# Input normed by token tile before it is turned, low-rank and attention gates with high and low columns side by side, compression inputs stored in order

## The chip, the cores and the metric

The program runs on one core of a Trainium2 chip. The metric is the device time of one execution in microseconds (us), the median of three executions; less is better. The core's engines are named as in the profile: PE (TensorE) multiplies, its weight loads are PEld; DVE (VectorE), ACT (ScalarE) and POOL (GpSimd) compute on tiles; SP (SyncE) issues most of the DMAs.

## What is computed

Two transformer-like blocks over 512 tokens of 1024 channels, in fp32. The first block has a gated linear attention layer (GLA) and a sparse attention layer (NSA), the second a stick-breaking attention with a pooling branch. Cut to what the change touches:

```python
def rms_norm(x, g):
    y = xf * lax.rsqrt(jnp.mean(xf * xf, axis=-1, keepdims=True) + NORM_EPS)
    return (y * g.astype(jnp.float32)).astype(x.dtype)

# layer 0, GLA: w_in is 1024 x 3088, 16 of its columns are the low-rank gate
h = rms_norm(x, pre_norm[0])
q, k, v, glr, z = split(h @ w_in)
gk = log_sigmoid(glr @ w_gk_up + b_gk) / 16
...
# layer 1, NSA: 48 gate columns; k and v compressed over blocks of 32 tokens
gates = sigmoid(gl + b_gate)                  # 512 x 48
kcmp = compress(kc, pe_k, ck_w1, ck_w2)       # 31 blocks, 4 groups
vcmp = compress(vc, pe_v, cv_w1, cv_w2)
s = einsum('bghtd,bgcd->bghtc', qb, kcmp)     # then softmax over blocks
...
```

## The kernel before

**How a product is made.** Each fp32 operand is kept as a high part (rounded to the type fp32r, in `w_hi`, `act_hi`) and a low part (the rest, in `w_lo`, `act_lo`). A product of fp32 accuracy takes three matmuls: high by high, low by high, high by low. Activations stand channels first: `act_hi` and `act_lo` are [128, 8, 512], eight slices k of 128 channels by 512 tokens. Weights are streamed in chunks of 256 columns (1 MB), numbered through the whole program: chunk 0 is `C_GLR`, 1 and 2 are `C_Q`, 3 and 4 `C_K`, 27 is `C_GL`, 28 to 31 `C_NQ`. Chunk c goes through buffer c % 2 of `raw`, `w_hi` and `w_lo`: SP loads it, once the low part of the chunk two back is done (`lo_done`), ACT makes the high part in two halves (`split_high`, L654), POOL the low part (`split_low`, L581), PE waits for each half (`weights_ready`) and writes PSUM banks 2u and 2u+1 (u = c % 2), ACT or DVE takes the banks and frees them (`bank_free`). The first chunks are handled apart.

**Order.** Every engine runs its own list in the order of the code and waits on semaphores. Nothing is scheduled by a planner; the order is written out by hand.

**The start.** SP loads x in two halves by channels (L400), then eleven small vectors (L404), `w_up`, and three chunks (L418). PE turns the raw x, eight slices of four 128x128 transposes (L1279), DVE copies them to `xT` (L1805). ACT squares x by token (L782); the sums are spread over all partitions by small matmuls on PE (L1287), and ACT makes `rstd` from them (L681, L682). Then, slice by slice, DVE makes `tmp` = xT * gain * rstd (L1822), ACT rounds it to `act_hi` (L691), DVE subtracts to `act_lo` (L1787). PE follows the slices (loop at L1292 on): for each k three matmuls of the low-rank chunk, which is loaded and multiplied 128 columns wide though 16 are used (L1296), and four of the first query chunk (L1305); the 16 matmuls with that chunk's low part come at the end (L1310). DVE makes both low parts of chunks 0 and 1 (`first_low`, L1813). The next product, chunk 2, has the gate's second factor in its middle: four matmuls with a contraction of 16 rows (`low_rank_up`, L1321).

**NSA.** `kv_high` (L862, ACT) and `kv_low` (L2031, DVE) split the gathered keys or values `kv_tok2` into `kv_hi` and `kv_lo`, which the compression's matmuls read (L1443). In both, elements are walked in the order group, block, position: `kv_tok2` is read in memory order, `kv_hi` and `kv_lo` are written with a step of 512 bytes between neighbours. Between `kv_low` and the values' arrival ACT copies the value banks to `kv_tok2` (L897). The gates' chunk C_GL is loaded whole, its 48 columns take three matmuls for each k (L1480), ACT applies bias and sigmoid (L921), PE turns the result (L1496), DVE copies it (L2072). The compressed scores (`c_score`, L1508) are 16 matmuls with a contraction of 64 rows and 32 result columns for each of four j, into banks 4 and 5; the two groups of a pair use the upper and lower half of the partitions.

## Time and profile before

| what | us |
|---|---|
| median of three executions | 1302.6 (1301.8 to 1305.51) |
| the profiled execution, whole | 1305.59 |
| its span in the trace | 1303.8 |
| PE busy within the span | 1258.7 (97%) |
| ACT, DVE, POOL busy | 576.2, 652.9, 400.4 |
| mean granted PE clock | 0.985 of full speed |

The trace shows the instructions of the profiled execution, from the start of its span. A group of matmuls is given its busy time with overlaps, so the spacing of starts, not the duration, says what one costs. "PEclk" is the clock that PE was granted, 1.00 for 2.4 GHz and 0.50 for 1.2 GHz. The idle time in brackets stands before the instruction on its own engine, with what ended it.

### The profile page before, as it was taken

The page shows a single profiled execution, that of the slowest core. Times are in us where ns is not written, and L with a number is a line of the kernel's source. Part 1 is how long each engine was busy: PE and PEld are TensorE (multiplying, and loading weights), DVE is VectorE, ACT ScalarE, POOL GpSimd, SP SyncE. Part 2 cuts the span into 40 slices and gives each one's busy share as a digit, 9 for nine tenths or more (in the row PEclk, how much of TensorE's full clock was granted, in tenths as well). Part 3 has the DMA queues.
Part 4 walks back from the last instruction along what each step waited for, and adds up shares of the span by engine and source line. Part 5 has one row for each costly group of instructions (what it writes and reads, how often), then busy time and mean ns, then how long its engine had stood idle before and what let it go on. Part 6 is the DMA issues. An engine that isn't in the chain of part 4 may idle for free.

```text
span 1303.8 us, 19513 instructions
## 1 busy us (share of the span) xinstructions
PE 1258.7 (97%) x7802; PEld 1040.4 (80%) x7802; DVE 652.9 (50%) x1212; ACT 576.2 (44%) x1086; POOL 400.4 (31%) x194
## 2 busy tenths in 40 slices
PE   6999998999989999999999999999999999999998
PEld 5799875998877765656699988888887788888898
DVE  6297534577815547698747033333333391102534
ACT  4435312353532137788846344445354411434333
POOL 1453411305652212010020422222222354444441
PEclk8999998999999999999999999999999999999999
DMA  5524500715465311110013232222111223333221
GB/s 172 181 77 144 179 1 33 241 55 162 130 133 94 77 38 42 24 34 2 1 33 98 69 94 65 65 65 65 61 60 60 80 97 97 97 98 109 80 86 65
DMA packets 130209, 109.68 MB, mean 84 GB/s; under 512 B 36162, under 2 KB 127424, under 8 KB 130128
## 3 DMA queue, kind: packets, MB, share of 16 engines
q1 hardware_dynamic: 130128, 108.54, 28.0%
q8 instruction: 58, 0.95, 0.3%
q14 instruction: 23, 0.19, 0.0%
HBM read 106.43 MB, written 2.10 MB: 83 GB/s over the span
## 4 chain that ended last, share of the span: by engine, by line
PE 69%; issue 17%; POOL 7%; DVE 4%; ACT 2%; DMA 0%; POOLq 0%; DVEq 0%; ACTq 0%
PE banks L1153 33%; POOL w_lo L581 6%; PE banks L1144 6%; PE banks L1176 5%; PE banks L1703 3%; PE banks L1555 3%; PE banks L1572 3%; PE banks L1587 3%; PE banks L1610 2%; PE banks L1241 2%; PE banks L1666 2%; PE banks L1717 1%; PE banks L1747 1%; PE banks L1120 1%; DVE w_lo L1813 1%
## 5 line engine op out<-in xcount | busy, mean ns | idle before, releaser
L581 POOL TENSOR_TENSOR w_lo<-raw,w_hi 128x1024 fp32r<-128x1024 f32 x158 | 389.8, 2488 | 811.8 <-ACT w_hi L654 811.7
L1153 PE MATMUL banks<-act_hi,w_hi 128*128 128x512 f32 x704 | 280.9, 399 | 2.1 <-POOL w_lo L581 2.1
L1153 PE MATMUL banks<-act_lo,w_hi 128*128 128x512 f32 x704 | 276.5, 393 | 0.0
L1153 PE MATMUL banks<-act_hi,w_lo 128*128 128x512 f32 x704 | 276.5, 393 | 0.0
L654 ACT ACTIVATE w_hi<-raw 128x1024 fp32r<-128x1024 f32 x168 | 168.0, 1050 | 123.4 <-PE banks L1153 91.6
L1153 PEld LDWEIGHTS banks<-act_hi,w_hi 128*128 128x128 f32 x704 | 133.6, 190 | 32.3 <-issue 5.0
L1153 PEld LDWEIGHTS banks<-act_lo,w_hi 128*128 128x128 f32 x704 | 133.3, 189 | 28.4
L1153 PEld LDWEIGHTS banks<-act_hi,w_lo 128*128 128x128 f32 x704 | 133.3, 189 | 28.2 <-issue 1.4
L1144 PE MATMUL banks<-w_hi,act_hi 128*128 128x256 f32 x384 | 109.4, 285 | 1.6 <-POOL w_lo L581 1.6
L1144 PE MATMUL banks<-w_hi,act_lo 128*128 128x256 f32 x384 | 108.8, 283 | 0.0
L1144 PE MATMUL banks<-w_lo,act_hi 128*128 128x256 f32 x384 | 108.8, 283 | 0.0
L968 ACT ACTIVATE prob<-prob,wstat 128x128 f32<-128x128 f32 (+3 forms) x128 | 70.8, 554 | 34.4 <-DVE wstat L2120 34.2
L2229 DVE TENSOR_TENSOR tmp<-banks,zh 128x512 f32<-128x512 f32 x8 | 5.5, 692 | 141.4 <-PE banks L1717 141.4
L1144 PEld LDWEIGHTS banks<-w_hi,act_hi 128*128 128x128 f32 x384 | 73.7, 192 | 2.1 <-issue 1.1
L1144 PEld LDWEIGHTS banks<-w_lo,act_hi 128*128 128x128 f32 x384 | 73.7, 192 | 0.0
L1144 PEld LDWEIGHTS banks<-w_hi,act_lo 128*128 128x128 f32 x384 | 73.7, 192 | 0.0
L1572 PEld LDWEIGHTS banks<-ident,prob 128*128 128x128 f32 x320 | 35.9, 141 | 33.3 <-issue 25.4
L1176 PE MATMUL banks<-w_hi,act_hi 128*128 128x256 f32 x192 | 56.4, 294 | 3.9 <-DVE act_lo L1787 2.3
L2120 DVE CUSTOM_DVE_ANT_0 prob<-banks,key_mask 128x128 f32<-128x128 f32 (+3 forms) x128 | 57.1, 484 | 3.7 <-PE banks L1555 3.5
L1176 PE MATMUL banks<-w_lo,act_hi 128*128 128x256 f32 x192 | 55.6, 289 | 0.0
L1176 PE MATMUL banks<-w_hi,act_lo 128*128 128x256 f32 x192 | 55.5, 289 | 0.0
L1572 PE MATMUL banks<-ident,prob 128*128 128x128 f32 x320 | 48.5, 282 | 5.7 <-ACT probT L981 3.8
(378 smaller groups left out, 2431.8 us busy)
## 6 DMA issues: line engine op xcount, KB each, us to landing
raw<-w_in SPq DMA_DIRECT2D x32, 1024.0 KB, 5.7
raw<-gla_w_in SPq DMA_DIRECT2D x13, 1024.0 KB, 5.4
raw<-nsa_w_in SPq DMA_DIRECT2D x32, 256.0 KB, 4.5
raw<-nsa_w_in SPq DMA_DIRECT2D x7, 1024.0 KB, 5.2
...
```

What stands on the lines that cost most here:

```text
L581: pool.tensor_tensor(w_lo[:, u, k], raw[:, u, k], w_hi[:, u, k].bitcast(F32), ALU.subtract).then_inc(lo_done, 1)
L654: act.activation(w_hi[:, u, k], raw[:, u, k], ACT.Copy).then_inc(hi_done, 1)
L968: act.activation(p, p, ACT.Exp, scale=-1.0, bias=wstat[:, u % 4, 0, half:half + 1], accum_out=wstat[:, u % 4, 1, half:half + 1]).then_inc( ...
L1144: mm = pe.matmul(b[:, t * CW:(t + 1) * CW], x[:, k, tok], w[:, u, k, :], start=(k == 0 and n == 0), stop=(k == KT - 1 and n == 2))
L1153: mm = pe.matmul(b[:], w[:, u, k, m * P:(m + 1) * P], x[:, k, :], start=(k == 0 and n == 0), stop=(k == KT - 1 and n == 2))
L1176: mm = pe.matmul(zone, x[:, k, tok], w[:, u, k, :], start=(start and n == 0), stop=(stop and n == 2), skip_group_check=True)
L1241: mm = pe.matmul(bank[2 * u + m][:, tok], w[:, u, k, m * P:(m + 1) * P], x[:, k, tok], start=(half == 0 and k == 0 and n == 0), stop=(k == ...
L1555: mm = pe.matmul(bank[2 * (u % 2) + half][:, 0:keys], qT[rows, i, t * P:(t + 1) * P], kT[rows, i // 4, 0:keys], start=True, stop=True)
L1572: mm = pe.transpose(bank[4 + half][:, k * P:(k + 1) * P], prob[:, u % 3, half, k * P:(k + 1) * P], ident[:])
L1587: mm = pe.matmul(bank[6][half * NDH:(half + 1) * NDH, 0:P], v_tok2[:, k, w, g * NDH:(g + 1) * NDH], probT[:, u % 2, half, k * P:(k + 1) * ...
L1703: mm = pe.matmul(blocks(z_banks, a, st, skip=jt - st), (tri_r if jt == st else minus_r)[:], blocks(part, a, jt), start=False, stop=(jt == ...
L2120: last = dve.tensor_tensor_reduce(prob[:, u % 3, half, 0:keys], bank[2 * (u % 2) + half][:, 0:keys], key_mask[:, S - keys:S], -1.0, -NEG, ...
```

## The change

It has four parts, and all the rest of the program stays as it was.

1. **The start.** x is loaded by token tile (four DMAs), the small vectors are issued from ACT's queue. ACT squares a token tile as it comes and makes one factor for each token (`x_root`); DVE scales the tile in place of tokens (`xn_tok`); PE turns the normed tiles, one pass of 32 transposes, into all eight banks, which are then read where they stand: ACT writes `act_hi` from the bank times the gain, DVE `act_lo` from the bank times the gain less `act_hi`. Ahead of that PE does 28 transposes of a constant tile whose result nobody reads. POOL, not DVE, makes the low part of chunk 1.
2. **The low-rank gate.** Its 16 columns (32 are loaded, 128 KB) stand as 32 high and 32 low columns in `glr_w`; one matmul with `act_hi` makes both partial results on 64 rows, one with `act_lo` adds to the first 32. `w_up` holds its 16 rows twice, with zeros between, so that the second factor's contraction of 64 rows also adds the two.
3. **The attention gates** in the same way: 64 columns are loaded, high and low side by side in `w_hi`; the two halves are added by a matmul with `pair_ident` that also turns them; bias by DVE, then the sigmoid by ACT.
4. **Compression.** `kv_hi` and `kv_lo` are walked in their own memory order and `kv_tok2` is read with a step of 8 elements (32 bytes). `kcmp2` holds the compressed keys of a pair of groups as two diagonal blocks, so that `c_score` is eight matmuls of 128 rows and 64 columns.

```diff
@@ sync @@
-            for half in range(2):
-                sp.dma_start(x_tok[:, :, half * S:(half + 1) * S],
...
+            for t in range(TT):
+                sp.dma_start(x_tok[:, t], A["x"][t * P:(t + 1) * P, :]).then_inc(x_landed[t], 16)
+            sp.dma_start(glr_raw[:], cols(w1, G_R, 32)).then_inc(glr_landed, 16)
...
+                        for half, landed in enumerate((first_landed, raw_landed[1])):
+                            k = slice(KT // 2 * half, KT // 2 * (half + 1))
+                            sp.dma_start(raw[:, 1, k], cols(m, at)[:, k]).then_inc(landed, 16)
...
+                elif c0 == C_GL:
+                    sp.wait_ge(lo_done, 2 * C_GL - 2)
+                    sp.dma_start(raw[:, C_GL % 2, :, 0:NDH], cols(m, at, NDH)).then_inc(raw_landed[C_GL % 2], 16)
@@ gpsimd @@
+            pool.memset(w_up[0:64, :], 0.0)
...
-            pool.wait_ge(lo_done, 2 * C_Q + 2)
-            split_range(C_Q + 1, C_KC)
+            split_low(C_Q, 1)
+            pool.wait_ge(lo_done, 2 * C_K)
+            split_range(C_K, C_KC)
...
+                    pool.tensor_tensor(w_hi[:, u, k, NDH:2 * NDH], raw[:, u, k, 0:NDH], w_hi[:, u, k, 0:NDH].bitcast(F32),
+                                       ALU.subtract).then_inc(lo_done, 1)
@@ scalar @@
+            for tiles in (range(3), range(3, 4)):
+                for t in tiles:
+                    act.wait_ge(x_landed[t], 16)
+                    ins = act.activation(sq_junk[:, t], x_tok[:, t], ACT.Square, accum_out=x_sum[:, t:t + 1])
...
+                link(act.activation(x_root[:, t], x_sum[:, t], ACT.Ln, scale=1.0 / D, bias=eps_col[:]))
+                act.activation(x_root[:, t], x_root[:, t], ACT.Exp, scale=-0.5).then_inc(start_rooted, 1)
+            act.wait_ge(glr_landed, 16)
+            act.activation(glr_w[:, :, 0, :], glr_raw[:], ACT.Copy).then_inc(hi_done, 2)
...
+            act.wait_ge(first_landed, 16)
+            first_high(1, 0)
+            act.wait_ge(vec_ready, 1)
+            for k in range(KT):
+                act.wait_ge(start_turned, k + 1)
+                act.activation(act_hi[:, k], start_bank(k), ACT.Copy, scale=vcol("pre0", k)).then_inc(act_hi_done, 1)
+                if k == 2:
+                    act.wait_ge(raw_landed[1], 16)
+                    first_high(1, 1)
+            act.wait_ge(raw_landed[0], 32)
+            first_high(0, 0)
+            first_high(0, 1)
...
-            act.activation(glr_t[:], bank[1][0:16, :], ACT.Copy).then_inc(bank_free[1], 1)
+            act.activation(glr_t[0:64, :], bank[1][0:64, :], ACT.Copy).then_inc(bank_free[1], 1)
             act.sem_inc(bank_free[0], 1)
...
-                    last = act.activation(by_block(kv_hi, part), kv_even(part), ACT.Copy)
+                    last = act.activation(kv_hi[:, part], kv_even(part), ACT.Copy)
...
-            act.activation(gates_t[:], bank[2 * u + 1][0:48, :], ACT.Sigmoid, bias=gate_bias[:]).then_inc(bank_free[2 * u + 1], 1)
+            act.activation(gate_parts[:], bank[2 * u + 1][:], ACT.Copy).then_inc(bank_free[2 * u + 1], 1)
...
-            untaken(C_NQ, 2)
+            untaken(C_NQ)
+            act.wait_ge(gate_summed, 1)
+            act.activation(gates[:].rearrange("p t n -> p (t n)"), gates[:].rearrange("p t n -> p (t n)"), ACT.Sigmoid)\
+                .then_inc(gate_ready, 1)
+            untaken(C_NQ + 1)
@@ tensor @@
+            for n in range(N_WARM):
+                pe.transpose(bank[7][:, n % 4 * P:(n % 4 + 1) * P], ones[:], ident[:])
...
+            for t in range(TT):
+                pe.wait_ge(start_scaled, t + 1)
+                for k in range(KT):
+                    mm = pe.transpose(start_bank(k)[:, t * P:(t + 1) * P], xn_tok[:, t, k * P:(k + 1) * P], ident[:])
...
+                mm = pe.matmul(bank[1][0:64, :], glr_w[:, k].rearrange("p a n -> p (a n)"), act_hi[:, k, :], start=(k == 0),
+                               stop=(k == KT - 1))
...
+                if k == KT - 1:
+                    mm.then_inc(bank_full[1], 1)
...
+                    pe.matmul(bank[4 + h][:], w_up[0:64, h * P:(h + 1) * P], glr_t[0:64, :], start=True, stop=True)\
...
-                mm = pe.transpose(bank[7][:, t * 48:(t + 1) * 48], gates_t[:, t * P:(t + 1) * P], ident[0:48, 0:48])
+                mm = pe.matmul(bank[7][:, t * 48:(t + 1) * 48], gate_parts[:, t * P:(t + 1) * P], pair_ident[:], start=True, stop=True)
...
+                        mm = pe.matmul(bank[4][:, at:at + 2 * NCP], qT[:, 2 * j + ii, t * P:(t + 1) * P], kcmp2[:, j // 2, :],
+                                       start=True, stop=True)
@@ vector @@
+            for t in range(TT):
+                dve.wait_ge(start_rooted, t // 3 + 1)
+                dve.tensor_scalar(xn_tok[:, t], x_tok[:, t], x_root[:, t:t + 1], None, ALU.mult).then_inc(start_scaled, 1)
...
+                dve.wait_ge(act_hi_done, k + 1)
+                dve.scalar_tensor_tensor(act_lo[:, k], start_bank(k), vcol("pre0", k), act_hi[:, k].bitcast(F32), ALU.mult,
+                                         ALU.subtract).then_inc(h_ready, 1)
...
+            dve.wait_ge(gate_ready, 1)
```

Where instructions now stand, at three places. On PE, the start of its list before, up to the first matmuls of the products (`tok_squares` are the sums of squares):

```order
L1279 MATMUL banks<-ident,x_tok 128x128 x32
L1282 MATMUL banks<-ident,vec_rows 128x94
L1287 MATMUL banks<-ident,tok_squares 128x128 x8
L1296 MATMUL banks<-act_hi,w_hi 128x512
L1296 MATMUL banks<-act_hi,w_lo 128x512
L1296 MATMUL banks<-act_lo,w_hi 128x512
```

and now:

```order
L1333 MATMUL banks<-ident,ones 128x128 x28
L1335 MATMUL banks<-ident,vec_rows 128x94
L1340 MATMUL banks<-ident,xn_tok 128x128 x32
L1362 MATMUL banks<-act_hi,w_hi 128x512
L1362 MATMUL banks<-act_hi,w_lo 128x512
L1362 MATMUL banks<-act_lo,w_hi 128x512
```

The turning moved behind the norm, the constant transposes stand where the turning stood, and the sums' matmuls are gone. On PE, the end of this first stage before, with the waits:

```order
L1310 MATMUL banks<-act_hi,w_lo 128x512 [waits lo_done]
L1310 MATMUL banks<-act_hi,w_lo 128x512 x7
L1310 MATMUL banks<-act_hi,w_lo 128x512 [waits lo_done]
L1310 MATMUL banks<-act_hi,w_lo 128x512 x7
L1153 MATMUL banks<-act_hi,w_hi 128x512 [waits lo_done,bank_free0]
```

and now (L1349 and L1350 are the low-rank gate's last two, L1211 the first of chunk 2):

```order
L1362 MATMUL banks<-act_lo,w_hi 128x512
L1349 MATMUL banks<-act_lo,glr_w 32x512
L1350 MATMUL banks<-act_hi,glr_w 64x512
L1211 MATMUL banks<-act_hi,w_hi 128x512 [waits lo_done,bank_free0]
L1211 MATMUL banks<-act_hi,w_lo 128x512
```

The 16 matmuls between the low-rank gate and chunk 2 are gone from there, so its last result stands directly ahead of the wait for `bank_free0`. On ACT, from the table load on, before:

```order
L676 ACT_TABLE_LOAD
L782 ACTIVATE sq_junk,tok_squares<-x_tok 128x512 x8
L681 ACTIVATE rstd<-banks,eps_col 128x512
L682 ACTIVATE rstd<-rstd 128x512
L654 ACTIVATE w_hi<-raw 128x1024 x2
L691 ACTIVATE act_hi<-tmp 128x512 x8
L791 ACTIVATE glr_t<-banks 16x512
```

and now, behind eleven DMA issues:

```order
L703 ACT_TABLE_LOAD
L806 ACTIVATE sq_junk,x_sum<-x_tok 128x1024 x3
L811 ACTIVATE x_root<-x_sum,eps_col 128x3
L812 ACTIVATE x_root<-x_root 128x3
L806 ACTIVATE sq_junk,x_sum<-x_tok 128x1024
L811 ACTIVATE x_root<-x_sum,eps_col 128x1
L812 ACTIVATE x_root<-x_root 128x1
L814 ACTIVATE glr_w<-glr_raw 128x8x32
L819 ACTIVATE w_hi<-raw 128x1024
L826 ACTIVATE act_hi<-banks,vec 128x512 x3
L819 ACTIVATE w_hi<-raw 128x1024
L826 ACTIVATE act_hi<-banks,vec 128x512 x5
```

The norm's factors come in two steps ahead of the first weights, and the second half of chunk 1's high part stands behind the third slice.

## Rows read from the trace of the kernel before

**Rows 1.** Waits of PE, 0 to 60 us: in total, times, longest.

```profile
PE banks L1279 <- DMA x_tok<-x: 6.3, 1, 6.3
```

**Rows 2.** Timeline of the start: begins, lasts (us), engine, line, operation [idle before].

```profile
0.81 1.28 ACT L676 ACT_TABLE_LOAD   x1 [0.81 <-PEq L2366]
...
1.86 0.81 SPq L404 DMA_DIRECT2D vec_rows<-pre_norm  x2
...
5.50 0.25 SPq L404 DMA_DIRECT2D vec_rows<-gla_head_norm  x1
...
4.95 0.10 POOL L574 MEMSET rstd<- 128x1 f32 x1
...
20.20 0.77 PE L1296 MATMUL banks<-act_hi,w_hi 128*128 128x512 f32 x1 [4.78 <-DVE act_lo L1787]
...
34.31 0.59 ACT L791 ACTIVATE glr_t<-banks 16x512 f32<-16x512 f32 x1 [5.86 <-PE banks L1296]
...
35.02 3.79 PE L1310 MATMUL banks<-act_hi,w_lo 128*128 128x512 f32 x16
38.64 0.39 PE L1153 MATMUL banks<-act_hi,w_hi 128*128 128x512 f32 x1
```

**Rows 3.** Groups by line, 0 to 38.7 us: busy us, mean ns, idle before.

```profile
L1822 DVE SCALAR_TENSOR_TENSOR tmp<-xT,vec,rstd 128x512 f32<-128x512 f32 x8 | 6.0, 752 | 0.7 <-ACT rstd L682 0.5
...
L581 POOL TENSOR_TENSOR w_lo<-raw,w_hi 128x1024 fp32r<-128x1024 f32 x2 | 4.8, 2400 | 30.9 <-ACT w_hi L654 30.9
```

**Rows 4.** Stretches: length, busy us of PE, PEld, DVE, ACT, POOL, PE clock, DMA.

```profile
7.00:8.00 1.00, 1.00 (x6) 1.00 (x5) 0.58 (x1) 1.00 (x4) 0.00 (x0) 1.00 1.06 383
11.00:12.00 1.00, 1.00 (x11) 1.00 (x10) 1.00 (x2) 0.47 (x2) 0.00 (x0) 1.00 1.09 372
23.00:24.00 1.00, 1.00 (x4) 0.81 (x3) 1.00 (x2) 0.35 (x1) 0.00 (x0) 0.50 1.05 359
```

**Rows 5.** Nearest prices: timeline of ACT, then a DVE group by shape.

```profile
265.99 1.05 ACT L741 ACTIVATE y_tok<-x_tok 128x1024 f32<-128x1024 f32 x1
...
267.48 0.20 ACT L707 ACTIVATE x_root<-x_root 128x1 f32<-128x1 f32 x1
...
L2135 DVE TENSOR_SCALAR prob<-prob,wstat 128x512 f32<-128x512 f32 x16 | 7.8, 486 | 2.4 <-DVE wstat L2132 1.1
```

**Rows 6.** Line L1321 (ns min/median/max, first and last start), a stretch behind it.

```profile
L1321 PE MATMUL banks<-glr_t,w_up x8: 587/588/692, 44.2 to 47.3; 16*128 16x512 f32 x8
...
48.30:51.70 3.40, 3.40 (x10) 2.67 (x9) 1.56 (x4) 0.00 (x0) 0.00 (x0) 0.51 1.09 386
```

**Rows 7.** Compression: timeline of ACT, DVE and PE.

```profile
314.69 3.90 ACT L862 ACTIVATE kv_hi<-kv_tok 128x1024 fp32r<-128x1024 f32 x2 [8.96 <-DVEq L2052]
...
330.86 2.01 ACT L654 ACTIVATE w_hi<-raw 128x1024 fp32r<-128x1024 f32 x2 [0.30 <-issue]
...
318.89 6.15 DVE L2031 TENSOR_TENSOR kv_lo<-kv_tok,kv_hi 128x1024 fp32r<-128x1024 f32 x2 [4.29 <-ACT kv_hi L864]
...
329.93 0.29 PE L1443 MATMUL banks<-w_hi,kv_hi 128*128 128x256 f32 x1
...
339.23 0.36 PE L1144 MATMUL banks<-w_hi,act_hi 128*128 128x256 f32 x1 [0.78 <-POOL w_lo L581]
```

**Rows 8.** Attention gates: line L1480, then timeline of ACT and PE.

```profile
L1480 PE MATMUL banks<-act_hi,w_hi x8: 397/397/401, 373.6 to 378.5; 128*48 128x512 f32 x8
...
378.31 2.00 ACT L654 ACTIVATE w_hi<-raw 128x1024 fp32r<-128x1024 f32 x2 [5.05 <-DMA raw<-nsa_w_in]
...
381.94 0.47 PE L1153 MATMUL banks<-act_hi,w_hi 128*128 128x512 f32 x1 [2.13 <-POOL w_lo L581]
```

**Rows 9.** Timeline of PE: values, gates turned, compressed scores.

```profile
394.54 1.89 PE L1490 MATMUL banks<-w2v,tmp 128*128 128x64 f32 x16
396.37 0.45 PE L1496 MATMUL banks<-ident,gates_t 48*128 48x48 f32 x4
...
409.63 1.97 PE L1508 MATMUL banks<-kcmpT,qT 64*128 64x32 f32 x32
```

232 lines of the change are left out of this document (117 added, 115 removed).

## The prediction

> **What bounds the kernel now.** I read the waits of PE first, then the timeline of the start, then the stretches with their clock, then the groups by line for prices. PE is the engine that ends the kernel: behind its first products it stands still only in short gaps, so what PE loses or saves there moves the end one for one. Its two long waits are at the start: 6.3 us for x [rows 1] and, after turning, 4.78 us for the first low slice of the activations; the first product begins at 20.20, chunk 2 at 38.64 [rows 2]. Full-speed matmuls of 512 columns start 0.226 us apart (16 from 35.02 to 38.64, 3.62 / 16 [rows 2]). The 72 of the first stage would need 16.3 us; they take 18.4, since PE begins them at half clock: four starts in a microsecond at 23 us, clock 0.50 [rows 4]. That is 2.1 us lost.
>
> **The change part by part: the start.** Three chains meet at the first product.
>
> ACT: eleven DMA issues come ahead of its table load. SP's eleven run from 1.86 to 5.75 [rows 2], some 0.35 each, so on ACT from 0.8 to 4.6; the table load of 1.28 [rows 2] ends at 5.9. Three squares of 1024 columns at 1.05 and the roots: one square with its root is 1.69 us from 265.99 to 267.68 [rows 5], so the roots alone are 0.64, and three tiles are ready at 6.0 + 3.15 + 0.64 = 9.8, the fourth at 11.5. The 256 columns of `glr_raw` cost some 0.4 (a quarter of 1024 and its start-up, my estimate), half a chunk's high part 1.05, as the square of the same size: 12.9. POOL's half of the low part is 2.40 [rows 3]: 15.4.
>
> PE and DVE: constants are ready at 5.05 [rows 2], now with one memset more, 5.6. The 28 constant transposes go at the pace of today's first ones, seven in a microsecond [rows 4]: 4.0, to 9.6; the vectors' transpose, its copy and DVE's bias step make 10.8. Now DVE scales four tiles. No row has this; 512 columns scaled in SBUF take 0.49 [rows 5], so 1024 at most 0.97 and less by one start-up: I take 0.8. With the price of the two-source form as upper bound (0.75 for 512 [rows 3], 1.5) it is 6.0 for four, not 3.2. So the last tile is scaled at 14.0 and its first slice turned at 14.2; `act_hi` (0.63, near 0.6 of a bank copy [rows 2]) makes 14.8, `act_lo` at 0.75 [rows 3] 15.6. The first product starts at **15.7**, where the two chains meet almost; from 15.0 (scaling at half my price) to 18.4 (at its bound, + 2.8). The later slices come 0.75 apart and PE needs 1.36 for each slice's six matmuls alone, so they stay ahead. The second half of the low part (behind the third slice, about 19.6) is needed after 32 matmuls, at 22.9.
>
> Then 64 matmuls, 8 less than now (8 x 0.226 = 1.8), at full clock: 14.5, to 30.2. That the clock is full is a choice. The clock row says 1.00 for all of the start, but the transposes of 7 to 8 us start at seven in a microsecond and those of 11 to 12 at eleven [rows 4]; PE went faster after 5 us that held transposes only. So transposes raise its pace here, and the new start has 60 of them, with idle stretches of a microsecond at most ahead of the product. The Trainium skill says the opposite: "TensorE: Matmul & The Clock Gate", Part 4, holds that transposes do not count as activity for the clock. By it the 28 constant ones would do nothing and the 2.1 us would stay lost; the pace in the two rows above speaks against it, and I give the rule a chance of its own below.
>
> A new wait: chunk 2 needs bank 0 free, which ACT signals after its copy of the low-rank result, 0.59 [rows 2]. Today 16 matmuls (L1310) cover it: the copy starts at 34.31 and chunk 2 at 38.64. Now the low-rank matmul is the last one, and PE waits for the copy and the hand-overs on both sides of it, which I put at 0.2 together: **0.8**. ACT is free by then. Chunk 2 thus starts at 31.0, not 38.64: **-7.6** (4.5 for the earlier start, 1.8, 2.1, less 0.8). What was queued behind chunk 2 is covered: its high part follows the slices on ACT (about 23), its low part on DVE is done at 25.4. The ACT copy of the first queries now stands behind chunk 3's high part, needed only when chunk 3 ends its wait 15 us later: nothing.
>
> **The second factor.** The eight instructions of L1321 keep their columns, so their time. Behind them the clock is 0.51 over the 3.4 us from 48.3 to 51.7 [rows 6], after 3 us of matmuls that use 16 rows: half of it, 1.6 us or so, is lost. With 64 rows the array is used four times as much. No row shows 64-row matmuls of this length; gain between 0 and 1.6. I take **-1.6**, since nothing else but these rows of 16 stands ahead of the fall.
>
> **Compression.** ACT's two `kv_hi` take 3.90, DVE's two `kv_lo` 6.15; behind them come the value copies, and the next chunk's high part starts at 330.86 [rows 7]. POOL's four halves follow that, and PE waits for them: 0.78 at 339.23 is one of three such waits [rows 7]. 128x1024 in plain order is 1.05 on ACT [rows 5] against 1.95. The high part cannot start before the product ahead of it ends, at 329.93 [rows 7]: at most 0.9 is to be had, and it is had if the chain shortens by a microsecond. Bounds 0 and -0.9; I take **-0.9**, since only one of three streams keeps a step. The Trainium skill speaks against this part: "SBUF — State Buffer", under "Door 1: The DMA port swizzle", says that consecutive accesses in one 16-byte line run at full rate and each new line costs; the new order reads at 32-byte steps, so by the page reading would cost what writing costs now. The trace has no such read. By it this term is 0 and the sum 0.9 smaller.
>
> **Gates.** Three matmuls for each of eight k, whose first ones start at 373.6 to 378.5 [rows 8] (0.70 for three, 0.233 each), become two: 1.9 less on PE. But behind them PE waits 2.13 us, to 381.94, for a chain that starts with chunk 28's DMA, for which ACT waited 5.05 us [rows 8]. The load is released by chunk 26's low part, which no edit touches. So the 1.9 turns into a longer wait: **0**, from -0.3 to +1.7 (if the wait of four us costs one more stretch at half clock). The turning was 4 instructions in 0.37; now 4 fp32 products, each two instructions as L1490, whose 16 take 1.83 [rows 9]: 8 x 0.114 = 0.9, **+0.5**. The new waits: ACT holds for DVE's sum before the sigmoid, with chunk 30's high part queued behind it; that comes some 5 us later (about 400 to 402, low part to 406) and PE needs it at the end of chunk 29, near 409. DVE waits for the sigmoid, to about 400, and its next input from PE comes at 403. Both are covered.
>
> **Compressed scores.** 32 instructions in 1.90 become 16 of L1490's shape, 16 in 1.83 [rows 9]: four times -0.07, **-0.3**. If they kept the pace of today's small ones it would be four times -0.95, so the bounds are -0.3 and -3.8. DVE's mask becomes one instruction, off the path.
>
> **Sum.** -7.6 - 1.6 - 0.9 + 0.5 - 0.3 = -9.9. Against the profiled execution: 1305.6 - 9.9 = 1295.7. That execution is 3.0 above the median of the three; the same shift on the median gives 1302.6 - 9.9 = **1292.7**.
>
> **The rivals.** (1) *Cold products*: the clock at the first product is half, as the skill's rule has it, and the sum is 2.1 smaller: 1294.8. For it: today's products did start cold. Against: the pace of the transposes. (2) *Late start*: scaling at its bound puts the product at 18.4, or the 1024 short pieces of `glr_raw` (128 bytes each) hold up the first half chunk behind them in the queue, for which ACT has 1 us of slack; 2.8 smaller, 1295.5; with the half clock after the second factor kept as well, 1297.1. (3) *The clock stays low behind the second factor* alone: 1294.3. (4) *Slower*: reading `kv_tok2` at steps of 32 bytes costs far more than writing at 512. PE needs the chunk's low part that ACT's chain releases, and each microsecond added to the chain from 314.69 to 330.86 [rows 7] moves PE by one. To lose the rest (9.0) the four instructions, now some 10 us with POOL beside them, must take 19: above 4.8 each. Then 1303 or more. Nothing in the profile speaks for such a price. (5) *The padding buys nothing*: if a matmul of 64 or 32 weight columns cost more than one of 128, the 16 low-rank ones would lose part of the 1.8; today's 48-column ones start 0.233 apart against 0.226, so 0.1 at most, and this lies within the forecast.
>
> **How the numbers follow.** Chances: forecast as summed 0.45 (1291.5 to 1293.9); (1) 0.13; (2) 0.17; (3) 0.13; (4) 0.03; better than the sum (faster scaling or scores) 0.09. A difference of about 0.3% (3.9 us) is what a measurement of this kernel can tell from no change. Only (4) and the tail of (2), with (1) and (3) joined, come near it: faster 0.90, same 0.07, slower 0.03. The range takes the forecast, (1), (3), and (2) with the half clock: 1289.5 to 1298.0.
>
> **What would show it.** First matmul of chunk 1 at 15.7 and of chunk 2 at 31.0, with an idle time of 0.8 before it that the low-rank copy ended; no stretch at 0.50 between 15 and 45; the gates' wait grown to some 4 us; the compression's first value wait gone or shorter by 0.9. The prediction is wrong if the product starts after 19, or if a stall of several us shows behind a PE that was made faster, in GLA's gate chain or at chunk 30.

## The result, and the profile of the changed kernel

| | kernel before | changed kernel |
|---|---|---|
| median of 4 runs, us | 1302.9 | 1293.6 |
| lowest to highest | 1301.8 to 1305.5 | 1292.9 to 1293.7 |
| profiled execution: time, span | 1305.6, 1303.8 | 1293.7, 1292.0 |
| PE busy in it, instructions | 1258.7, 7802 | 1248.8, 7738 |

The ratio of the changed kernel to the one before is 0.9925, with a 95% interval of 0.9907 to 0.9942: faster by 9.3 us. The forecast was 1292.7. The sign, the range and the size held. The terms held less well: one had the wrong sign, one was far too small, and the size of the largest turned out to be a matter of luck from one execution to the next.

In the waits of PE (the columns are: in total, times, longest) the transfer of x from [rows 1] is gone. PE now waits for POOL's constants at the start, and the second line is the wait behind the gates:

```profile
PE banks L1333 <- POOLq L586: 5.5, 1, 5.5
...
PE banks L1211 <- POOL w_lo L594: 3.8, 1, 3.8
```

The start in the timeline, against [rows 2]: the scaling of the four tiles, POOL's first low half, the turning (L1340), the first product (L1362), the copy of the low-rank result, and the first matmul of chunk 2 (L1211).

```profile
11.13 2.73 DVE L1874 TENSOR_SCALAR xn_tok<-x_tok,x_root 128x1024 f32<-128x1024 f32 x4
...
13.33 3.09 POOL L594 TENSOR_TENSOR w_lo<-raw,w_hi 128x1024 fp32r<-128x1024 f32 x1 [7.98 <-ACT w_hi L819]
...
12.03 3.69 PE L1340 MATMUL banks<-ident,xn_tok 128*128 128x128 f32 x32 [1.30 <-DVE xn_tok L1874]
...
16.57 0.50 PE L1362 MATMUL banks<-act_hi,w_hi 128*128 128x512 f32 x1 [0.86 <-DVE act_lo L1879]
...
31.46 0.59 ACT L835 ACTIVATE glr_t<-banks 64x512 f32<-64x512 f32 x1 [8.84 <-PE banks L1350]
...
31.54 0.50 PE L1211 MATMUL banks<-act_hi,w_hi 128*128 128x512 f32 x1
```

The first product begins 3.6 us earlier than before, chunk 2 7.1 earlier (38.64 [rows 2]). The stretches, with PE's clock behind POOL's share as in [rows 4], print it as full in all of them. The numbers in brackets count every instruction that reaches into a stretch, so they are more than the starts. The starts tell the pace: the constant transposes stand 0.213 us apart until 9.3 us and 0.109 behind it, the turning ones 0.109, the products at 23 us 0.23, where 0.43 stood before. So PE ran at half its pace up to 9.3 us, though the row prints 1.00 there too: ahead of its first change the clock row of these traces does not tell the pace. The last line is the stretch behind the second factor, 16 matmuls where ten stood at clock 0.51 [rows 6].

```profile
7.00:8.00 1.00, 1.00 (x6) 1.00 (x6) 0.00 (x0) 1.00 (x3) 0.00 (x0) 1.00 1.05 365
...
9.00:10.00 1.00, 1.00 (x9) 1.00 (x8) 0.00 (x0) 0.97 (x3) 0.00 (x0) 1.00 1.07 304
...
13.00:14.00 1.00, 1.00 (x11) 1.00 (x10) 1.00 (x3) 0.24 (x1) 0.67 (x1) 1.00 1.10 348
...
23.00:24.00 1.00, 1.00 (x6) 0.68 (x5) 1.00 (x2) 0.00 (x0) 0.00 (x0) 1.00 1.08 376
...
40.90:44.30 3.40, 3.40 (x16) 2.79 (x16) 2.01 (x4) 0.00 (x0) 0.00 (x0) 1.00 0.52 185
```

The compression in the timeline, against [rows 7]. Two `kv_hi` take 4.29, where they took 3.90, the two `kv_lo` 6.25 (6.15), and the wait at the first value product (331.58) is still 0.79.

```profile
306.60 4.29 ACT L916 ACTIVATE kv_hi<-kv_tok 128x1024 fp32r<-128x1024 f32 x2 [8.17 <-DVEq L2110]
...
311.18 6.25 DVE L2090 TENSOR_TENSOR kv_lo<-kv_tok,kv_hi 128x1024 fp32r<-128x1024 f32 x2 [4.67 <-ACT kv_hi L918]
...
323.19 2.01 ACT L681 ACTIVATE w_hi<-raw 128x1024 fp32r<-128x1024 f32 x2 [0.30 <-issue]
...
331.58 0.35 PE L1202 MATMUL banks<-w_hi,act_hi 128*128 128x256 f32 x1 [0.79 <-POOL w_lo L594]
```

The gates, against [rows 8], and the turn and the scores, against [rows 9]: PE now waits 3.77 before chunk 29, behind the same DMA; the turn is eight instructions, a group of scores 16.

```profile
370.37 2.00 ACT L681 ACTIVATE w_hi<-raw 128x1024 fp32r<-128x1024 f32 x2 [4.77 <-DMA raw<-nsa_w_in]
...
363.48 7.68 SPq L497 DMA_DIRECT2D raw<-nsa_w_in  x8
...
373.99 0.47 PE L1211 MATMUL banks<-act_hi,w_hi 128*128 128x512 f32 x1 [3.77 <-POOL w_lo L594]
...
388.31 1.04 PE L1563 MATMUL banks<-pair_ident,gate_parts 128*128 128x48 f32 x8
...
401.92 1.89 PE L1573 MATMUL banks<-kcmp,qT 128*128 128x64 f32 x16
```

PE is seldom free for long, so the distance between the same instruction on PE in two traces tells what each stretch gave. This table is that difference (changed minus before, at the moments of before), step by step; the last column is a second profiled execution of the same changed kernel, which comes below as `e12_changed_again`.

| stretch of the kernel before | predicted | changed | changed, again |
|---|---|---|---|
| start, to chunk 2 (38.64) | -7.6 | -7.10 | -4.93 |
| second factor, to the V stream (76.8) | -1.6 | -1.43 | -1.46 |
| to the first compression product (329.9) | 0 | +0.37 | +0.90 |
| compression, to 339.2 | -0.9 | +0.51 | +0.50 |
| to chunk 29 (381.9) | 0 | -0.30 | -0.28 |
| gates turned, to 396.7 | +0.5 | +0.39 | +0.18 |
| compressed scores, to 516.2 | -0.3 | -0.89 | -0.88 |
| one wait of PE at 519.0 | 0 | -1.82 | -1.81 |
| half clock behind it, to 523.7 | 0 | -0.92 | -0.93 |
| to the end (1285.9) | 0 | -0.46 | -0.47 |
| sum | -9.9 | -11.65 | -9.18 |

What the changed kernel loses on the way to the first compression product is for the most part one wait: at 242.0 us PE waits 1.96 for POOL's low half (the same instruction waited 1.08 in the kernel before), and ahead of that half ACT waits for a load of `gla_w_out`. In the first trace a half-clock stretch that is 3.4 us shorter pays for part of it.

### The profile page after: what moved, and what is told of

Its sections match the earlier page's. It is cut to its first block, busy times and chain, and to the rows that moved or that the text cites. A ratio compares the mean times of both kernels' runs of the same rounds, so it can differ in the third digit from the quotient of the medians.

```text
span 1292.0 us, 19356 instructions
## 1 busy us (share of the span) xinstructions
PE 1248.8 (97%) x7738; PEld 1032.5 (80%) x7738; DVE 639.3 (49%) x1194; ACT 574.5 (44%) x1082; POOL 398.8 (31%) x196
## 4 chain that ended last, share of the span: by engine, by line
PE 69%; issue 18%; POOL 7%; DVE 4%; ACT 2%; POOLq 0%; DVEq 0%; ACTq 0%
PE banks L1211 33%; PE banks L1202 6%; POOL w_lo L594 6%; PE banks L1234 5%; PE banks L1767 3%; PE banks L1619 3%; PE banks L1651 3%; PE banks L1636 3%; PE banks L1299 2%; PE banks L1674 2%; PE banks L1730 2%; PE banks L1781 1%; PE banks L1811 1%; PE banks L1178 1%; ACT prob L1026 1%
## 5 line engine op out<-in xcount | busy, mean ns | idle before, releaser
L1211 PE MATMUL banks<-act_hi,w_hi 128*128 128x512 f32 x704 | 280.2, 398 | 3.9 <-POOL w_lo L594 3.8
L1211 PE MATMUL banks<-act_lo,w_hi 128*128 128x512 f32 x704 | 275.7, 392 | 0.0
L1211 PE MATMUL banks<-act_hi,w_lo 128*128 128x512 f32 x704 | 275.4, 391 | 0.0
L681 ACT ACTIVATE w_hi<-raw 128x1024 fp32r<-128x1024 f32 (+1 forms) x164 | 162.8, 1042 | 125.9 <-PE banks L1211 90.9
L1211 PEld LDWEIGHTS banks<-act_hi,w_hi 128*128 128x128 f32 x704 | 133.0, 189 | 34.0 <-issue 6.6
L1211 PEld LDWEIGHTS banks<-act_hi,w_lo 128*128 128x128 f32 x704 | 133.1, 189 | 28.4 <-issue 1.4
L1211 PEld LDWEIGHTS banks<-act_lo,w_hi 128*128 128x128 f32 x704 | 132.8, 189 | 28.3
```

The lines of the kernel that those rows point to most:

```text
L681: act.activation(w_hi[:, u, k, 0:n], raw[:, u, k, 0:n], ACT.Copy).then_inc(hi_done, 1)
L1211: mm = pe.matmul(b[:], w[:, u, k, m * P:(m + 1) * P], x[:, k, :], start=(k == 0 and n == 0), stop=(k == KT - 1 and n == 2))
```

## The experiments

Each kernel was run beside the kernel before on the same chip. The intervals of the ratios reach 2.2 to 3.8 us to either side. One cause shows in the traces: summed over the microseconds of a trace, the share of the clock that was not granted comes to between 8.0 and 19.8 us (before 19.8, changed 11.5, its second execution 13.5; the last 1 to 2 us of it fall at the end, where PE is done), mostly in steps of 1.7, and a step comes or goes when the work around it shifts a little. So the verdicts below rest on the traces, and the ratios stand beside them.

**The constant transposes left out.**

```
-N_WARM = 28
+N_WARM = 0
```

> The changed kernel without its 28 constant transposes at the start (N_WARM = 0), all else the same. Theory of the prediction (transposes raise PE's pace, and the full clock at the first product comes from them): without them the 32 turning transposes run at the half pace (0.177 us each, so the tail of the turning ends some 0.3 us later) and the first products start at half clock; the first stage takes up to 2.1 us more, time about 1295.7. Rival (the 32 turning transposes alone are enough, or the products warm the engine as fast): first product at 16.57 or a little earlier, chunk 2 at 31.5, time unchanged, 1293.6. By the rule of the Trainium skill, TensorE: Matmul & The Clock Gate, Part 4 (transposes do not count as activity), taking them away changes nothing either: also 1293.6.

Measured: 1293.5 us, ratio 0.9930 (0.9908 to 0.9952). The first product begins at 17.98, 1.41 later than in the changed kernel, and at full clock. The loss is in the turning. Its transposes in two parts (least, median and longest duration in ns, first and last start in us), two stretches, and DVE's scaling:

```profile
L1340 PE MATMUL banks<-ident,xn_tok x16: 404/421/447, 11.7 to 15.0; 128*128 128x128 f32 x16
...
L1340 PE MATMUL banks<-ident,xn_tok x15: 272/272/273, 15.3 to 16.8; 128*128 128x128 f32 x15
...
14.00:15.00 1.00, 1.00 (x7) 1.00 (x6) 0.00 (x0) 0.00 (x0) 1.00 (x1) 1.00 1.13 344
...
16.00:17.00 1.00, 1.00 (x11) 0.88 (x9) 0.00 (x0) 0.55 (x1) 0.15 (x1) 1.00 0.27 70
...
10.85 2.74 DVE L1874 TENSOR_SCALAR xn_tok<-x_tok,x_root 128x1024 f32<-128x1024 f32 x4
```

The transposes start 0.213 us apart up to 15.0 and 0.109 from 15.3 on, with nothing on PE but transposes. They bring PE to its pace by themselves, here as at 9.3 us of the changed kernel. The DMA traffic, which falls over the same microseconds (344 to 70 GB/s), is not the cause: in the changed kernel the spacing is 0.109 at 13 us beside 348 GB/s. So the theory's mechanism stands, and its place and size were wrong: 1.4 us in the turning, where 0.3 was expected, and nothing in the products, which would have been warm without the constant transposes. The Trainium skill's "TensorE: Matmul & The Clock Gate", Part 4, has it that transposes do not count as activity; the trace does not agree, with 0.213 us between two starts before 15.0 and 0.109 behind it.

The 1.4 us hold against the first trace of the changed kernel alone. In the executions that are the commoner ones (below, under `e12_changed_again`) the changed kernel's first product begins at 18.5 or later, so this kernel, in its one trace, is ahead of them: its fourth tile is scaled from 12.84 on, before POOL begins at 13.38. The constant transposes pay only where they end early.

The median did not rise by 1.4; this kernel's trace lost 8.3 us to the low clock in all, less than either of the changed kernel's, so the part given up at the start was made up by such steps later. The medians alone would have hidden the 1.4.

**The second factor's 64 rows alone, in the kernel before.**

```
-pe.matmul(bank[4 + h][:], w_up[:, h * P:(h + 1) * P], glr_t[:], start=True, stop=True).then_inc(up_full, 1)
+pe.matmul(bank[4 + h][:], w_up[0:64, h * P:(h + 1) * P], glr_t[0:64, :], start=True, stop=True).then_inc(up_full, 1)
```

> The kernel before with one part of the change alone: the second factor's four matmuls contract 64 rows in place of 16 (rows 16 to 63 of both operands are zeros set at the start, so the result is the same; the load of w_up moves behind chunk 2's load). Theory of the prediction: no stretch at half clock follows the second factor (before: granted clock 0.51 from 48.3 to 51.7), and the V stream, which starts 38.14 us behind chunk 2 before, starts 36.5 behind it; time -1.6 against the kernel before, 1301.3. Rival (the rows don't matter, the fall has to do with the start): the half-clock stretch stays, 1302.9.

Measured: 1300.7 us (10 runs), ratio 0.9980 (0.9963 to 0.9997). The second factor's line and the stretch behind it:

```profile
L1324 PE MATMUL banks<-glr_t,w_up x8: 589/589/693, 44.8 to 47.9; 64*128 64x512 f32 x8
```

```profile
48.30:51.70 3.40, 3.40 (x15) 2.73 (x15) 2.14 (x4) 0.00 (x0) 0.00 (x0) 1.00 1.09 386
```

A matmul with 64 rows takes the 589 ns of one with 16 [rows 6], but behind eight of them PE stays at full clock: 15 matmuls where ten stood. From chunk 2 to the V stream 1.58 us are gained. Not all of it arrives: at 205 us this kernel is 0.57 behind the kernel before, because another half-clock stretch has come between 162 and 169. The mechanism is shown, and so is that a stretch of low clock avoided in one place can come back in another.

**The compression's order undone, in the changed kernel.**

```
-last = act.activation(kv_hi[:, part], kv_even(part), ACT.Copy)
+last = act.activation(by_block(kv_hi, part), kv_even(part), ACT.Copy)
```

> The changed kernel with one part undone: the compression's high and low parts are written block by block again (the view of kv_tok2 read in storage order, kv_hi and kv_lo written at a step), all else as changed. What it computes is the same. Theory of the prediction (one ordered side saves 0.45 us for each of ACT's two kv_hi instructions, so this undo costs up to 0.9): kv_hi two in 3.9 + 0.9 = 4.8 us or more, the next stage 0.9 later against the key compression's start, time +0.9, about 1294.5. Rival (a read at a 32-byte step costs what a write at a step costs; the changed kernel's two take 4.29, before they took 3.90): the two go back to 3.90, the value product's stretch from the first compression product to the first value product shrinks by 0.4 us, time -0.4, about 1293.2. Both are too small for the time itself to decide; the trace's durations and the distance on PE from the first compression product to chunk 24's first product (9.81 us in the changed kernel, 9.30 in the kernel before) decide.

Measured: 1294.5 us, ratio 0.9929 (0.9904 to 0.9955), too coarse for the question. The group by line tells it, four `kv_hi` of this kernel:

```profile
L920 ACT ACTIVATE kv_hi<-kv_tok 128x1024 fp32r<-128x1024 f32 x4 | 7.8, 2054 | 8.4 <-DVEq L2115 8.4
```

and of the changed kernel:

```profile
L916 ACT ACTIVATE kv_hi<-kv_tok 128x1024 fp32r<-128x1024 f32 x4 | 8.5, 2184 | 8.2 <-DVEq L2110 8.2
```

Writing in order and reading at a step is 0.13 us slower per instruction than the reverse, and PE gains 0.3 to 0.4 by the undo, from the first compression product to 339.2 us of the kernel before (measured against the second execution of the changed kernel, whose start is the same; the same undo between e4 and e6 below gives 0.4). The rival is right: this part of the change costs 0.3 to 0.5 us. "SBUF — State Buffer", under "Door 1: The DMA port swizzle", of the Trainium skill leads one to expect no gain from it, and the trace agrees (2.18 us an instruction against 2.05).

**The gates undone, in the changed kernel.**

```
-if k:
-    pe.matmul(bank[2 * u + 1][0:NDH, :], w_hi[:, u, k, 0:NDH], act_lo[:, k, :], start=False, stop=False)
-mm = pe.matmul(bank[2 * u + 1][:], w_hi[:, u, k, 0:2 * NDH], act_hi[:, k, :], start=(k == 0), stop=(k == KT - 1))
...
+for n, (w, x) in enumerate(((w_hi, act_hi), (w_lo, act_hi), (w_hi, act_lo))):
+    mm = pe.matmul(bank[2 * u + 1][0:48, :], w[:, u, k, 0:48], x[:, k, :],
+                   start=(k == 0 and n == 0), stop=(k == KT - 1 and n == 2))
```

> The changed kernel with one part undone: the attention gates again as 24 matmuls of 48 columns, their weights loaded 256 wide and split on POOL into w_lo, four transposes in place of the four fp32 products, sigmoid before the turn. What it computes is the same. Theory of the prediction (PE's 1.9 us are swallowed by the wait for chunk 29's low part, whose chain starts at a DMA that the gates don't touch): PE's wait before chunk 29 goes from 3.76 back to about 2.1 us, chunk 29 starts within 0.3 us of where it does now relative to the value compression, and the turn behind it is 0.4 to 0.5 shorter: time -0.2 to -0.5, about 1293.3. Rival (the gates' products bound that stretch): chunk 29 starts 1.9 later, time +1.4, 1295.0.

Measured: 1292.7 us, ratio 0.9924 (0.9895 to 0.9953). The wait before chunk 29:

```profile
374.49 0.47 PE L1191 MATMUL banks<-act_hi,w_hi 128*128 128x512 f32 x1 [1.69 <-POOL w_lo L590]
```

It is 1.69 in place of 3.77, so the 24 products run in time that the 16 leave idle: chunk 29 begins 0.1 earlier against the value compression than in the changed kernel. The turn behind it is 0.40 shorter. And the stretch at half clock that follows PE's wait (from 374 us in the changed kernel) is not there in this kernel, which is 1.6 more. That is not one trace's: it follows in all eight profiles in which PE waited 3.6 to 4.6 us here, and in one of the six in which it waited 1.4 to 2.3, the kernel before. So the gates' part of the change costs 0.3 in what PE does and, where the stretch follows, 1.6 in clock. The prediction had this as the upper bound of the term (+1.7); in the comparison of the two first profiles it is hidden, since that execution of the kernel before had the stretch too.

**The compressed scores undone, in the changed kernel.**

```
-mm = pe.matmul(bank[4][:, at:at + 2 * NCP], qT[:, 2 * j + ii, t * P:(t + 1) * P], kcmp2[:, j // 2, :],
-               start=True, stop=True)
+for half in range(2):
+    rows = slice(half * NDH, (half + 1) * NDH)
+    g = 2 * (j // 2) + half
+    mm = pe.matmul(bank[4 + half][:, (2 * t + ii) * NCP:(2 * t + ii + 1) * NCP],
+                   qT[rows, 2 * j + ii, t * P:(t + 1) * P], kcmpT[rows, g * NCP:(g + 1) * NCP], start=True, stop=True)
```

> The changed kernel with one part undone: the compressed scores again as 32 matmuls of 64 rows into two banks for each of four steps, and DVE's mask in two instructions. What it computes is the same. Theory of the prediction (16 matmuls of 128 rows cost nearly what 32 of 64 rows cost, since an fp32 product is two instructions): each of the four score groups 0.07 us longer, PE's distance from chunk 30's first product behind the scores to the last group's end +0.3, time +0.3. Rival (from the changed kernel's trace, in which the group of chunk 30 took 1.70 where the one before took 1.90, and PE gained 1.0 us between 389 and 474): this undo gives the 1.0 back, time +1.0, about 1294.6.

Measured: 1296.5 us, ratio 0.9948 (0.9930 to 0.9965), the slowest of the kernels that have the new start. Each of the four groups takes 1.91 us, where the changed kernel's take 1.70 once and 1.81 three times; with what lies between them PE falls 0.7 behind. Then comes what neither theory had. The timeline at 506 to 512 us, in the middle of the selected attention:

```profile
506.46 2.31 DVE L2195 TENSOR_TENSOR wstat<-wstat,gates 128x2 f32<-128x2 f32 x1
...
508.93 2.30 DVE L2198 TENSOR_SCALAR prob<-prob,wstat 128x256 f32<-128x256 f32 x1
...
506.38 4.69 POOL L594 TENSOR_TENSOR w_lo<-raw,w_hi 128x1024 fp32r<-128x1024 f32 x2 [10.15 <-ACT w_hi L680]
...
511.28 0.70 PE L1638 MATMUL banks<-ident,prob 128*128 128x128 f32 x4 [1.67 <-DVE prob L2198]
```

and the same place of the changed kernel:

```profile
505.78 0.16 DVE L2193 TENSOR_TENSOR wstat<-wstat,gates 128x2 f32<-128x2 f32 x1
506.09 2.33 DVE L2196 TENSOR_SCALAR prob<-prob,wstat 128x256 f32<-128x256 f32 x1
...
505.89 4.76 POOL L594 TENSOR_TENSOR w_lo<-raw,w_hi 128x1024 fp32r<-128x1024 f32 x2 [10.35 <-ACT w_hi L681]
```

An instruction of two columns (`wstat`) takes 0.16 us, and 2.31 where POOL's low half began 0.08 before it. In the old form POOL begins just ahead of `wstat`: that one is held for POOL's first half and the scaling of `prob` for its second, and PE stands still for 1.67. In the new form POOL begins 0.11 behind the start of `wstat`, so one of the two gets through, and PE does not wait. The wait is there in all four profiles with the old scores (1.65 to 1.67), and in none of the ten with the new ones. In the new form a later `wstat` is held for 1.26 us and two small waits follow (0.19 and 0.22), so 0.4 is given back. By this undo the scores are worth 0.7 + 1.8 - 0.4 = 2.1 us and not 0.3, and two thirds of it is how DVE's work falls against POOL's. The half-clock stretch behind the wait at 519.0 is no part of it: of the four profiles with the old scores only the kernel before has it.

**One wait on POOL.** The same hold decides the start. In two of the changed kernel's relatives above the first product had begun at 18.5 to 18.7.

```
+pool.wait_ge(start_scaled, TT)
 split_low(C_Q, 1)
```

> The changed kernel with one wait more: POOL begins its first half of chunk 1's low part only when DVE has scaled the fourth token tile. Nothing else differs. In the changed kernel's own trace DVE began the fourth tile 0.15 us before POOL began, and the four took 2.73; in two of the kernels run since (nothing of their start differs) the constant transposes ended 0.6 to 0.8 later, POOL began first, DVE's four took 4.83 and the first product began at 18.5 to 18.7 in place of 16.57. Theory (DVE's scaling in SBUF cannot run beside POOL's two-input instruction, whichever starts first holds the other up): with the wait DVE's four take 2.7 in any run, POOL begins at 13.9 to 14.7, its half takes about 2.4, the first product begins between 16.5 and 17.3; time equal to the changed kernel's best or up to 1.5 below its median. Rival (DVE's longer scaling came from late data of x or from DMA traffic, not from POOL): with POOL held back the fourth tile still takes some 2.8 in a run whose constant transposes end late, and the first product begins at 18.5 or later.

Measured: 1292.5 us, ratio 0.9917 (0.9896 to 0.9938). Its start:

```profile
10.86 0.25 PE L1336 MATMUL banks<-ident,vec_rows 94*128 94x94 f32 x1
...
11.51 2.73 DVE L1875 TENSOR_SCALAR xn_tok<-x_tok,x_root 128x1024 f32<-128x1024 f32 x4
...
14.33 2.47 POOL L594 TENSOR_TENSOR w_lo<-raw,w_hi 128x1024 fp32r<-128x1024 f32 x1 [8.97 <-DVE xn_tok L1875]
...
16.95 0.50 PE L1363 MATMUL banks<-act_hi,w_hi 128*128 128x512 f32 x1 [0.86 <-DVE act_lo L1880]
```

**The changed kernel once more**, with no edit:

> The changed kernel itself once more, to see how its start comes out in another execution and what its median is beside the others of this call. Theory (a race between DVE's fourth scaling and POOL's first low half, which the pace of the constant transposes decides: early in two of the executions of this start seen so far, at 16.2 and 16.6, late in three, at 18.5 to 18.7): the first product begins either near 16.5 with DVE's four in 2.7, or near 18.7 with DVE's four in 4.8; median 1293 to 1296. Rival (the late starts belong to the kernels in which they were seen): 16.57 again and 1293.6.

Measured: 1293.4 us (6 runs), ratio 0.9934 (0.9916 to 0.9953). Its start:

```profile
11.25 0.25 PE L1335 MATMUL banks<-ident,vec_rows 94*128 94x94 f32 x1
...
11.90 4.83 DVE L1874 TENSOR_SCALAR xn_tok<-x_tok,x_root 128x1024 f32<-128x1024 f32 x4
...
13.47 2.72 POOL L594 TENSOR_TENSOR w_lo<-raw,w_hi 128x1024 fp32r<-128x1024 f32 x1 [8.12 <-ACT w_hi L819]
...
18.75 0.50 PE L1362 MATMUL banks<-act_hi,w_hi 128*128 128x512 f32 x1 [0.86 <-DVE act_lo L1879]
```

Here POOL begins before DVE's fourth tile (13.89), and DVE's four take 4.83, not 2.73; the fourth ends 0.5 behind POOL's instruction, having taken 2.85 in place of 0.75. In the first trace DVE was ahead by 0.2 (13.12 against 13.33). In e7 the fourth tile begins at 13.50, behind POOL's usual 13.3 to 13.5, but POOL is held back and the four take 2.73 again. Both theories of e7 and e12 are decided: it is POOL's instruction, not the data, and the late start belongs to no particular kernel. What sets the sides is the constant transposes' pace, which doubles at 9.3 us in one execution and only at 11.0 in the other; the vectors' transpose queues behind them, at 10.48 or 11.25, and DVE's copy of it and the scaling behind that. Of the eight profiled kernels with this start unaltered two had the early one, six the late one (in one of the six, e10 below, it is the third tile that is held, and the product begins at 19.21). So the usual gain of the start is 4.9, not 7.1. "Trainium Architecture — The Big Picture", under "What this means for kernel authors", of the Trainium skill names this hold: VectorE and GpSimd share a pair of ports under an exclusive lock. The trace agrees: one scaling of 0.75 us is longer by 2.1.

**The start and the second factor alone**: the changed kernel with compression, gates and scores undone as in the three diffs above.

> The start and the second factor's 64 rows alone: the changed kernel with the compression's order, the gates and the compressed scores all undone. What it computes is the same. Theory of the prediction (start -7.6, second factor -1.6, the other three together -0.7): chunk 2 starts near 31.5 (33.7 where POOL begins first), the V stream 36.7 behind it, time -9.2 against the kernel before. From the runs (compression's order costs 0.45, scores bring 1.0, gates and their turn about 0): -0.6 against the sum of all, 1294.2 with the early start, 1296.3 with the late one. Rival (the other three parts carry part of the gain): above 1297.

Measured: 1293.0 us, ratio 0.9933 (0.9916 to 0.9951). Chunk 2 starts at 33.52 (the late start), the V stream 36.69 behind it. So the start and the rows carry the whole of the measured difference, and the other three parts together none that can be measured: by the traces +0.4 for the compression, +0.3 and usually 1.6 of clock for the gates with their turn, and -2.1 for the scores. The rival falls.

**Chunk 29's load from two queues.** The wait of 3.77 is the largest in the changed kernel behind the start. SP's queue shows 0.96 for each of the pieces of 256 KB.

```
-for h in range(2):
+for h in range(1 if c0 + j == C_NQ else 2):
...
+act.wait_ge(lo_done, 2 * (C_NQ - 1))
+for g in range(2):
+    act.dma_start(raw[:, C_NQ % 2, :, P + g * NDH:P + (g + 1) * NDH], cols(w2, N_Q + g * CW + NDH, NDH))\
+        .then_inc(raw_landed[C_NQ % 2], 16)
```

> The changed kernel, where two of the four loads of chunk 29 (the first attention queries) are issued by ACT in place of SP, right when the buffer is free. SP's queue takes 0.96 us for each of them, ACT's high part of chunk 29 waited 4.77 us for them, and PE then 3.76. Theory (the chain in front of chunk 29 is: buffer free, four issues in a row of 3.8 us, landing, high part, low part): landing 1.9 us earlier, PE's wait before chunk 29 goes from 3.76 to about 1.9, time -1.9, about 1291.7; and the gates' eight products fewer, which the wait swallowed, are now part of the gain. Rival (the transfer's bandwidth or its latency bounds, not the issues): the landing stays, wait 3.7, time unchanged.

Measured: 1295.8 us, ratio 0.9941 (0.9920 to 0.9962). The wait is longer:

```profile
377.61 0.77 PE L1215 MATMUL banks<-act_hi,w_hi 128*128 128x512 f32 x1 [4.58 <-POOL w_lo L594]
```

The theory fell, the rival stands. The DMA engines move some 220 GB/s in both kernels, after 240 to 280 in the first two microseconds. SP, freed of two pieces, sends chunk 30's sooner, and these can take part of that rate from chunk 29's; that this is why the wait grew is argued, no run separates it.

**Chunk 29's load in two halves of k.** If the transfer bounds, it must begin earlier.

```
-sp.wait_ge(lo_done, 2 * (c0 + j - 1))
+parts = 2 if c0 + j == C_NQ else 1
+for part in range(parts):
+    k = slice(KT // parts * part, KT // parts * (part + 1))
+    sp.wait_ge(lo_done, 2 * (c0 + j - 1) - (parts - 1 - part))
...
+            sp.dma_start(raw[:, u, k, h * P + g * NDH:h * P + (g + 1) * NDH],
+                         cols(m, at_col, NDH)[:, k]).then_inc(raw_landed[u], 16)
```

> The changed kernel, where the load of chunk 29 (the first attention queries) is issued in two halves of k: the first four pieces when POOL has used the first half of the buffer (2.35 us earlier than now), the last four when it has used the second. e8 showed that two queues do not help: the 256-byte pieces move at 217 to 290 GB/s whoever issues them, and a megabyte takes the time. Theory (the transfer bounds, so an earlier begin is what helps): ACT's high part of chunk 29 begins 2.0 us earlier than the 370.37 of the changed kernel relative to the value compression, PE's wait before chunk 29 goes from 3.76 to about 1.8, time -2.0. Rival (eight smaller pieces cost more than the earlier begin gives, or the last piece's latency bounds): wait 3.3 or more, time within 0.5 of the changed kernel.

Measured: 1291.5 us, ratio 0.9918 (0.9899 to 0.9938).

```profile
371.05 2.01 ACT L684 ACTIVATE w_hi<-raw 128x1024 fp32r<-128x1024 f32 x2 [2.39 <-DMA raw<-nsa_w_in]
...
374.69 0.47 PE L1214 MATMUL banks<-act_hi,w_hi 128*128 128x512 f32 x1 [1.42 <-POOL w_lo L597]
```

ACT waits 2.39 in place of 4.77, PE 1.42 in place of 3.77, and no half-clock stretch follows. Counted from the compression, PE is 2.4 us ahead of the second execution of the changed kernel at chunk 29 and 3.8 at 389 us, where the missing stretch is in it. As expected, and more.

**What the traces point to, together.** First with the two queues, then with the halved load in their place. Both have the compression's order of before, ACT's first high part ahead of the low-rank one, and at the start:

```
-N_WARM = 28
+N_WARM = 24
...
+pool.wait_ge(start_scaled, TT)
 split_low(C_Q, 1)
...
 for t in range(TT):
     dve.tensor_scalar(xn_tok[:, t], x_tok[:, t], x_root[:, t:t + 1], None, ALU.mult).then_inc(start_scaled, 1)
+    if t == 0:
+        dve.wait_ge(vec_full, 1)
+        dve.tensor_copy(vec[:], bank[0][:, 0:NVEC]).then_inc(vec_ready, 1)
```

> What the traces point to, together: the two queues of e8, the compression's order of before (e1), and at the start 24 constant transposes in place of 28, DVE's copy of the vectors between the first and the second scaling in place of ahead of all, ACT's first high part ahead of the low-rank one, and POOL's first low part behind the fourth scaling (e7). What it computes is the same. Theory: first product at 16.0 (changed kernel 16.57 in its trace, 18.5 to 18.7 in two others of the same start), compression -0.45, chunk 29's wait -1.9: time about 3 us below the changed kernel, 1290.5. Rival (each gain is taken back by the next wait, as the eight gate products were): within 1 us of the changed kernel.

Measured: 1291.9 us, ratio 0.9909 (0.9891 to 0.9927). The first product begins at 16.10, as expected; the two queues took back 0.6 at chunk 29 (0.8 in e8).

> Together: the start of e9 (24 constant transposes, the vectors' copy between the first and second scaling, POOL's first low part behind the fourth scaling), the compression's order of before, and the halved release of e10; not the two queues of e8. What it computes is the same. Theory: first product at 15.9 in every execution, chunk 2 at 30.9, compression -0.45, chunk 29's wait -2.0: 3.1 below the changed kernel with its early start and 5.2 below its late one, about 1290. Rival (the gain at chunk 29 is taken back at chunk 30): 1291.5, no better than e9.

Measured: 1286.1 us, ratio 0.9876 (0.9856 to 0.9896), 7.3 below the changed kernel on the same chip and the best of all. Its start and chunk 29:

```profile
11.29 2.07 DVE L1879 TENSOR_SCALAR xn_tok<-x_tok,x_root 128x1024 f32<-128x1024 f32 x3
...
13.45 2.54 POOL L602 TENSOR_TENSOR w_lo<-raw,w_hi 128x1024 fp32r<-128x1024 f32 x1 [8.10 <-DVE xn_tok L1879]
...
16.13 0.47 PE L1371 MATMUL banks<-act_hi,w_hi 128*128 128x512 f32 x1 [0.98 <-POOL w_lo L602]
...
369.96 0.47 PE L1220 MATMUL banks<-act_hi,w_hi 128*128 128x512 f32 x1 [2.27 <-POOL w_lo L602]
```

The first product now waits for POOL's low half. Chunk 2 starts 7.6 earlier than in the kernel before, the size forecast for the start; but that takes all of this start's edits, since with POOL's wait alone (e7) it is 6.75. More than the 5.2 expected comes from half-clock stretches that are gone (at 157 and 376 us against the second profile of the changed kernel).

## Why the prediction was right, and where its steps were not

The total and the sign were right. By steps:

- **The start, -7.6.** Measured -7.1 and, more often, -4.9. The first product was put at 15.7 and came at 16.57. Four sizes were off. The constant transposes were put at "seven in a microsecond", 4.0 us in all, by the (x6) and (x7) of the stretches, which count more than the starts; the starts stand 0.213 us apart, so that from the first of them to the vectors' transpose it is 5.0 us, and 5.8 in the second execution. Scaling cost 0.68 a tile (0.8 put), but begins only at 11.13 or 11.90 (10.8 put). The 32 turning transposes were not costed as a chain: they take 3.69, so the last tile's first slice is turned at about 15.0, not 14.2. POOL's half takes 3.09, not 2.40, beside DVE. Against that the low-rank copy, put at 0.8, cost 0.27: chunk 2 (31.54) starts 0.08 behind the copy's start and before its end, since ACT signals bank 0 without waiting for the copy. And the clock was full at the first product, as chosen: seven and eleven a microsecond are such counts too, by the starts it is 4.7 and 9.2, and the step between them, on which the choice rested, is real.
- **Rival 2, the late start.** It was given 0.17 and is the commoner case. The place (DVE's scaling) and the time (18.4; measured 18.5 to 19.2) were right, the mechanism was not: neither the price of the scaling nor the pieces of `glr_raw`, but DVE held by POOL. The part of the prediction that failed is the sentence that puts scaling at one price, as if POOL's neighbouring instruction were free; the constants' pace then decides which of the two comes first. With the late start the forecast by the text's own terms would have been 1295.4, where 1293.6 and 1293.4 were measured.
- **The cold clock, rival 1.** It fell; e2 shows where the warm-up is worth something, 1.4 us in the turning, and that the late start takes more than that back.
- **The second factor, -1.6.** Right: -1.43, and -1.58 by itself in e3. Rival 3 fell.
- **Compression, -0.9.** Wrong sign: +0.5. The failed step is the choice of -0.9 between its bounds, on the ground that one side only keeps a step. The read at a step costs 2.1 us where the write cost 1.95, and the chain grew.
- **Gates, 0, and their turn, +0.5.** In PE's work right: -0.3 and +0.4, with the wait grown to 3.77, as foretold (some 4). The clock behind that wait was put at its better end; e4 and the profiles beside it show that the worse one, 1.6 us, is usual behind so long a wait.
- **Scores, -0.3.** Too small in PE's own time (0.7 by the undo), and blind to the wait at 519 us (1.8, of which 0.4 comes back). The half-clock stretch behind it, gone from the changed kernel (0.9 in the table), is luck: the other three kernels with the old scores don't have it either. The profile of before showed the 1.65 us wait, but nothing in the text looked at what DVE did there.
- **The rest.** So the sum came out near for a reason that was not in it: in the usual execution the start gave 2.7 less and the compression 1.4 less than forecast, the stretch from the scores to 523.7 us gave 3.3 more. That these cancel is luck, and the forecast of size is right in part by it.

What stays open is how often each start comes in executions that were not traced, what makes the constant transposes' pace double at 8.6 us in one execution and at 11.0 in another, and what decides how much low clock there is between 155 and 250 us (5.1 to 8.5 us lost, in the traces with the new start).
